# ScalarE scales the routed token rows out of place, and TensorE combines the last expert pass by selector products

## What is computed

```python
def _moe(x, router_w, wg, wu, wd):
    xf = x.reshape(b * t, d)
    logits = (xf @ router_w).astype(jnp.float32)
    top_val, top_idx = lax.top_k(logits, TOP_K)           # TOP_K = 2 of N_EXPERTS = 8
    gates = jax.nn.softmax(top_val, axis=-1)
    combine = jnp.sum(jax.nn.one_hot(top_idx, N_EXPERTS) * gates[..., None], axis=1)
    y = jnp.zeros((b * t, d), jnp.float32)
    for e in range(N_EXPERTS):
        y = y + combine[:, e:e + 1] * _swiglu(xf, wg[e], wu[e], wd[e])
    return y
...
h = h + _moe(_rmsnorm(h, norm2_g[1]), ...)
y = _rmsnorm(h, final_norm_g)
```

## Time and profile before

| what | value |
|---|---|
| median of three runs | 1635.87 us (1633.38, 1635.87, 1636.98) |
| the profiled execution, its own time | 1633.93 us |
| its span, first to last instruction | 1632.1 us |
| PE busy | 1517.0 us, 93% |
| PE weight loads | 1318.9 us, 81% |
| DVE busy | 1283.1 us, 79% |
| ACT busy | 958.9 us, 59% |
| POOL busy | 222.5 us, 14% |
| DMA | 447.74 MB, 274 GB/s over the span |
| mean granted clock of TensorE | 0.964 of full speed |

### The profile page before, as it was taken

One profiled execution on the slowest core, in us unless ns is written; L12 is line 12 of the kernel. 1 busy time (PEld: TensorE's weight loads), 2 busy tenths in 40 slices (PEclk: granted clock), 3 DMA queues, 4 the chain that ended last, 5 costly groups with the idle time before them and its releaser, 6 DMA issues.

```text
span 1632.1 us, 21551 instructions
## 1 busy us (share of the span) xinstructions
PE 1517.0 (93%) x7811; PEld 1318.9 (81%) x7811; DVE 1283.1 (79%) x1279; ACT 958.9 (59%) x903; POOL 222.5 (14%) x235
## 2 busy tenths in 40 slices
PE   4958999999996889899999999999999999999993
PEld 4857999999985887688888888888888888888882
DVE  4898765544589758788888888888888888888885
ACT  3444243333344426677777777777777777777772
POOL 4354500001135406300000000000000000000001
PEclk8979999999997988999999999999999999999997
DMA  6114699435111536999999999999999999999993
GB/s 185 34 56 152 204 325 293 147 119 174 52 33 62 168 98 202 395 396 376 372 371 366 378 366 366 373 366 373 385 349 375 375 361 366 384 364 369 385 343 114
DMA packets 243728, 447.74 MB, mean 274 GB/s; under 512 B 8869, under 2 KB 93925, under 8 KB 243679
## 3 DMA queue, kind: packets, MB, share of 16 engines
q1 hardware_dynamic: 239568, 437.35, 75.4%
q0 software_dynamic: 2880, 9.56, 1.9%
q10 hardware_dynamic: 1231, 0.19, 0.1%
HBM read 421.43 MB, written 25.65 MB: 274 GB/s over the span
## 4 chain that ended last, share of the span: by engine, by line
PE 56%; issue 4%; DVE 2%; POOL 2%; ACT 2%; DMA 1%; SPq 0%; DVEq 0%; ACTq 0%; POOLq 0%
PE ps L1479 18%; PE ps L1481 18%; PE ps L1480 18%; PE ps L1766 1%; ACT w_hi L480 1%; POOL hn L724 1%; DVE xg_lo L1408 1%; POOL xg L727 1%; PE ps L1749 1%; POOL og L760 0%; DMA xg<-hn,row_i 0%; DMA og<-obuf,out_row_i 0%; DMA raw<-in_moe_w_gate_dram 0%; DVE w_lo L485 0%; PE ps L1650 0%
## 5 line engine op out<-in xcount | busy, mean ns | idle before, releaser
L485 DVE TENSOR_TENSOR w_lo<-raw,w_hi 128x2048 fp32r<-128x2048 f32 x336 | 769.4, 2292 | 139.4 <-ACT w_hi L480 137.6
L480 ACT ACTIVATE w_hi<-raw 128x2048 fp32r<-128x2048 f32 x336 | 643.6, 1916 | 141.1 <-PE ps L1481 132.4
L1479 PE MATMUL ps<-w_hi,xg_hi 128*128 128x512 f32 x896 | 356.9, 398 | 10.1 <-DVE w_lo L485 5.4
L1480 PE MATMUL ps<-w_lo,xg_hi 128*128 128x512 f32 x896 | 355.1, 396 | 0.0
L1481 PE MATMUL ps<-w_hi,xg_lo 128*128 128x512 f32 x896 | 354.7, 396 | 0.0
L1479 PEld LDWEIGHTS ps<-w_hi,xg_hi 128*128 128x128 f32 x896 | 169.1, 189 | 53.6 <-issue 7.8
L1481 PEld LDWEIGHTS ps<-w_hi,xg_lo 128*128 128x128 f32 x896 | 169.3, 189 | 40.7
L1480 PEld LDWEIGHTS ps<-w_lo,xg_hi 128*128 128x128 f32 x896 | 169.3, 189 | 39.8
L1479 PE MATMUL ps<-x_hi,w_hi 128*128 128x336 f32 x580 | 189.0, 326 | 11.3 <-DVE x_lo L1223 5.8
L1481 PE MATMUL ps<-x_hi,w_lo 128*128 128x336 f32 x580 | 187.1, 323 | 0.0
L1480 PE MATMUL ps<-x_lo,w_hi 128*128 128x336 f32 x580 | 186.7, 322 | 0.0
(11 more groups left out here) (236 smaller groups left out, 1878.8 us busy)
## 6 DMA issues: line engine op xcount, KB each, us to landing
raw<-in_moe_w_gate_dram SPq DMA_DIRECT2D x112, 1024.0 KB, 7.2
raw<-in_moe_w_up_dram SPq DMA_DIRECT2D x112, 1024.0 KB, 7.5
raw<-in_moe_w_down_dram SPq DMA_DIRECT2D x112, 1024.0 KB, 7.1
raw<-in_w_in_dram SPq DMA_DIRECT2D x12, 1024.0 KB, 5.0
raw<-in_ffn_w_gate_dram SPq DMA_DIRECT2D x11, 1024.0 KB, 6.1
raw<-in_ffn_w_up_dram SPq DMA_DIRECT2D x11, 1024.0 KB, 6.4
raw<-in_w_out_dram SPq DMA_DIRECT2D x8, 1024.0 KB, 9.8
obuf<-ones SPq DMA_DIRECT2D x15, 512.0 KB, 7.9
```

What stands on the lines that cost most here:

```text
L480: nc.scalar.activation(hi, r, ACT.Copy).then_inc(hi_done, 1)
L485: nc.vector.tensor_tensor(lo, r, hi.bitcast(F32), ALU.subtract).then_inc(lo_done, 1)
L1479: nc.tensor.matmul(out, a_hi, b_hi, start=start, stop=False)
L1480: nc.tensor.matmul(out, a_hi, b_lo, start=False, stop=False)
```

## The change

Three things are done.

1. `hn` is no longer scaled in place by POOL. ACT writes the scaled rows to another tile (`hs`, which is `og[:, 1]`, empty until the end) by three Copy activations with the 1/rms as scale, placed between its wait for `gap_done` and the Exp. POOL's scatters read `hs` and wait for these (`hn_scaled`) and for the rows; POOL no longer waits for PE's gather.
2. The last pass's output doesn't go through `obuf`. All six gathers of line 760 are issued at `o_early`. The higher rows which are of the last pass hold nothing of use then; their gate is set to zero (`early_gate`). POOL prepares, during the passes, the position of each token's higher row in the last chunk (`last_pos`), sends it through a small DRAM row to all partitions, and compares it with the partition's number: `sel_t` is 1 where slot s of the last chunk belongs to token t. After the last pass ACT and DVE split `D_` to `o_hi` and `o_lo`, and PE multiplies them by `sel_t`: 12 products of 112 x 512 into six banks. DVE adds these, times the gate, to `yt` in six pieces.
3. DVE waits for all six gathers (`og_early` at 96) and for `sel_t` ahead of its first addition, where it waited for three; it then does the first additions (three), the two `o_lo`, three additions for the higher rows, and the six pieces.

`pick_e` moves into a free part of `h`, to make room.

```diff
@@ -123,6 +123,7 @@
 
     xg = nc.dram_tensor("xg", (CHUNKS * P, D), F32, kind="Internal").ap()
     obuf = nc.dram_tensor("obuf", ((CHUNKS + 1) * P, D), F32, kind="Internal").ap()
+    last_row = nc.dram_tensor("last_row", (T,), F32, kind="Internal").ap()
     xg_chunks = xg.rearrange("(c p) d -> c p d", p=P)
     obuf_chunks = obuf.rearrange("(c p) d -> c p d", p=P)
 
@@ -203,6 +204,7 @@
         yt = sb("yt", [TT, 3, D], F32, moe)
         hn = sb("hn", [TT, 3, D], F32, moe)
         og = sb("og", [TT, 2, 3, D], F32, moe)
+        hs = og[:, 1]
         xg_hi = sb("xg_hi", [P, KD, P], F32R, moe)
         xg_lo = sb("xg_lo", [P, KD, P], F32R, moe)
         act_s = sb("act_s", [P, 512], F32, moe)
@@ -231,6 +233,13 @@
         out_row = sb("out_row", [TT, 2, 3], F32, moe)
         out_row_i = sb("out_row_i", [TT, 2, 3], I32, moe)
         out_gate = sb("out_gate", [TT, 2, 3], F32, moe)
+        last_base = sb("last_base", [TT, 1], F32, moe)
+        last_pos = sb("last_pos", [TT, 3], F32, moe)
+        early_gate = sb("early_gate", [TT, 3], F32, moe)
+        last_bc = h[:, KD - 1, :]
+        slot_id = sb("slot_id", [P, 1], F32, moe)
+        sel_t = sb("sel_t", [P, T], F32R, moe)
+        o_hi, o_lo = (x[:].rearrange("p k s -> p (k s)") for x in (xg_hi, xg_lo))
         cnt = sb("cnt", [P, NE], F32, moe)
         extra = sb("extra", [P, NE], F32, moe)
         before_e = sb("before_e", [P, NE, NE], F32, moe)
@@ -239,7 +248,7 @@
         n_chunks = sb("n_chunks", [P, NE], F32, moe)
         key = sb("key", [P, 2, NE], F32, moe)
         pick = sb("pick", [P, 6, 2 * NE], F32, moe)
-        pick_e = sb("pick_e", [P, 6, 2 * NE], F32, moe)
+        pick_e = h[:].rearrange("p k t -> p (k t)")[:, 2 * D:2 * D + 12 * NE].rearrange("p (i e) -> p i e", i=6)
         key_sum = sb("key_sum", [P, 1], F32, moe)
         eids_f = sb("eids_f", [P, 8], F32, moe)
         table_load = sb("table_load", [1, 1], F32, moe)
@@ -249,6 +258,7 @@
         SUM_BANK, TOKEN_SUMS = ps[:, 6, 0:T], ps[0:TT, 7, 0:3]
         G_, U_, T_, X0, X1 = (ps[:, i, :] for i in (0, 1, 2, 5, 6))
         D_ = ps[:, 3:5, :]
+        LAST_BANKS = [ps[:, i, :] for i in (0, 1, 2, 5, 6, 7)]
 
 
         landed = [sem(f"landed{i}") for i in range(RAW)]
@@ -276,7 +286,7 @@
         state_stored = sem("state_stored")
         gb_landed, hn_sq = sem("gb_landed"), sem("hn_sq")
         rwg_done, logits_done, hot_done, ranks_done = sem("rwg_done"), sem("logits_done"), sem("hot_done"), sem("ranks_done")
-        gap_done, exp_done, hn_done = (sem(n) for n in ("gap_done", "exp_done", "hn_done"))
+        gap_done, exp_done, hn_done, hn_scaled = (sem(n) for n in ("gap_done", "exp_done", "hn_done", "hn_scaled"))
         sel_ready = sem("sel_ready")
         routed, extra_done = sem("routed"), sem("extra_done")
         top_done, route_step = sem("top_done"), sem("route_step")
@@ -286,9 +296,9 @@
         g_done, u_done, e_silu, e_f, t_done, ft_hi_done, ft_lo_done, d_done = (
             sem(n) for n in ("g_done", "u_done", "e_silu", "e_f", "t_done", "ft_hi_done", "ft_lo_done", "d_done"))
         o_done, o_stored, o_early = sem("o_done"), sem("o_stored"), sem("o_early")
-        o_last = [sem(f"o_last{i}") for i in (0, 1)]
-        o_last_stored, og_early = sem("o_last_stored"), sem("og_early")
-        og_late = [sem(f"og_late{t}") for t in range(3)]
+        og_early = sem("og_early")
+        last_sent, last_landed, sel_t_done = sem("last_sent"), sem("last_landed"), sem("sel_t_done")
+        o_hi_done, o_lo_done, last_done = sem("o_hi_done"), sem("o_lo_done"), sem("last_done")
         out_rows_done, y_added = sem("out_rows_done"), sem("y_added")
         fin_sq, fin_out, stored = sem("fin_sq"), sem("fin_out"), sem("stored")
         dve_step, act_step, pool_step = sem("dve_step"), sem("act_step"), sem("pool_step")
@@ -556,11 +566,6 @@
 
             sp.wait_ge(o_stored, n_pass * 16 + 16)
             sp.sem_inc(o_early, 1)
-            last_chunk = obuf_chunks[ds(n_pass, 1)].rearrange("a p d -> p (a d)")
-            for i in (0, 1):
-                sp.wait_ge(o_last[i], 1)
-                sp.dma_start(last_chunk[:, 512 * i:512 * (i + 1)], o[:, 512 * i:512 * (i + 1)]
-                             ).then_inc(o_last_stored, 16)
             n_out = 0
             for t, r, m, name, row in PIECES:
                 if name != "meta":
@@ -718,15 +723,13 @@
                 link(nc.gpsimd.tensor_tensor(out, x[:, :, 0], x[:, :, 1], ALU.add))
 
             pool.wait_ge(filled, 16 * (2 * CHUNKS + 1))
+            pool.wait_ge(hn_scaled, 3)
             pool.wait_ge(rows_done, 1)
-            pool.wait_ge(gather_done, 2)
-            for t in range(3):
-                link(nc.gpsimd.tensor_scalar(hn[:, t, :], hn[:, t, :], nt[0:TT, t, 1:2], None, ALU.mult))
             for t in range(3):
                 for k in (0, 1):
                     nc.gpsimd.indirect_dma_start(
                         out=xg, out_offset=bass.IndirectOffsetOnAxis(ap=row_i[:, t, k:k + 1], axis=0),
-                        in_=hn[:, t, :], in_offset=None).then_inc(x_sent, 16)
+                        in_=hs[:, t, :], in_offset=None).then_inc(x_sent, 16)
             pool.wait_ge(x_sent, 16 * 6)
             pool.sem_inc(x_rows, 1)
 
@@ -762,12 +765,22 @@
                     in_offset=bass.IndirectOffsetOnAxis(ap=out_row_i[:, i, t:t + 1], axis=0)).then_inc(done, 16)
 
             pool.wait_ge(out_rows_done, 1)
+            link(nc.gpsimd.tensor_scalar(last_base[:], eids_f[0:TT, 6:7], -float(P), -float(P * NE), ALU.mult, ALU.add))
+            link(nc.gpsimd.tensor_scalar(last_pos[:], out_row[:, 1, :], last_base[:, 0:1], None, ALU.add))
+            pool.dma_start(last_row.rearrange("(p t) -> p t", p=TT), last_pos[:]).then_inc(last_sent, 16)
+            link(nc.gpsimd.tensor_scalar(early_gate[:], last_pos[:], 0.0, None, ALU.is_lt))
+            link(nc.gpsimd.tensor_tensor(early_gate[:], early_gate[:], out_gate[:, 1, :], ALU.mult))
+            link(nc.gpsimd.iota(slot_id[:], pattern=[[0, 1]], base=0, channel_multiplier=1,
+                                allow_small_or_imprecise_dtypes=True))
+            pool.wait_ge(last_sent, 16)
+            pool.dma_start(last_bc, last_row.rearrange("(a t) -> a t", a=1).broadcast_to([P, T])).then_inc(last_landed, 16)
+            pool.wait_ge(last_landed, 16)
+            nc.gpsimd.tensor_scalar(sel_t[:].rearrange("s (t p) -> s t p", t=3), last_bc.rearrange("s (p t) -> s t p", t=3), slot_id[:, 0:1], None, ALU.is_equal).then_inc(sel_t_done, 1)
+
             pool.wait_ge(o_early, 1)
-            for t in range(3):
-                gather_outputs(0, t, og_early)
-            pool.wait_ge(o_last_stored, 32)
-            for t in range(3):
-                gather_outputs(1, t, og_late[t])
+            for i in (0, 1):
+                for t in range(3):
+                    gather_outputs(i, t, og_early)
 
 
         def splitter(eng, split):
@@ -935,6 +948,9 @@
             token_squares(og[:, 0], [(t, 1) for t in range(3)], lambda t, i: act.wait_ge(evac, GROUP[("htok", t, 1)] + 1), hn_sq)
 
             act.wait_ge(gap_done, 1)
+            for t in range(3):
+                act.wait_ge(hn_done, 3 + t + 1)
+                nc.scalar.activation(hs[:, t, :], hn[:, t, :], ACT.Copy, scale=nt[0:TT, t, 1:2]).then_inc(hn_scaled, 1)
             nc.scalar.activation(gt[:, :, 1], gt[:, :, 0], ACT.Exp).then_inc(exp_done, 1)
 
             def gathered_hi(p):
@@ -986,10 +1002,10 @@
                 act.nop()
             n_pass = n_over + NE
             act.wait_ge(d_done, n_pass + 1)
-            act.wait_ge(o_early, 1)
-            nc.scalar.activation(o[:, 0:512], D_[:, 0, :], ACT.Copy).then_inc(o_last[0], 1)
-            token_squares(hn, [(t, i) for t in range(3) for i in (0, 1)],
-                          lambda t, i: act.wait_ge(y_added, 2 * t + i + 4), fin_sq)
+            for i in (0, 1):
+                nc.scalar.activation(o_hi[:, 512 * i:512 * (i + 1)], D_[:, i, :], ACT.Copy).then_inc(o_hi_done, 1)
+            token_squares(hn, [(t, i) for i in (0, 1) for t in range(3)],
+                          lambda t, i: act.wait_ge(y_added, 6 + 3 * i + t + 1), fin_sq)
 
 
         @block.vector
@@ -1441,19 +1457,27 @@
                     expert_pass(i + NE)
                 dve.nop()
             n_pass = n_over + NE
-            dve.wait_ge(og_early, 48)
+            dve.wait_ge(og_early, 96)
+            dve.wait_ge(sel_t_done, 1)
             for t in range(3):
                 nc.vector.scalar_tensor_tensor(yt[:, t, :], og[:, 0, t, :], out_gate[:, 0, t:t + 1], yt[:, t, :],
                                                ALU.mult, ALU.add).then_inc(y_added, 1)
-            dve.wait_ge(d_done, n_pass + 1)
-            nc.vector.tensor_copy(o[:, 512:1024], D_[:, 1, :]).then_inc(o_last[1], 1)
-            dve.wait_ge(y_added, 3)
+            for i in (0, 1):
+                dve.wait_ge(o_hi_done, i + 1)
+                cols = slice(512 * i, 512 * (i + 1))
```

(27 more changed lines are left out.)

## The result

The changed kernel took 1622.53 us (median of four, 1621.29 to 1623.11) beside 1635.91 us for the kernel before (median of four, 1633.38 to 1636.98): ratio 0.9919, 95% interval 0.9902 to 0.9937, some 13.4 us faster. Two repeats on other occasions gave 0.9939 (0.9924 to 0.9953) and 0.9927 (0.9914 to 0.9941), that is 1625.57 and 1623.52 us; over all three comparisons the means differ by 11.3 us (15 executions at 1623.5, 24 at 1634.8, either with a standard deviation of 1.7).

A forecast was written before the change was run, and what follows sets the result against it. The prediction took TensorE, busy nearly all the time, to bound the kernel. Pass 0, ACT's copies and the end summed to -7.3 + 0 - 1.5 = -8.8 us, forecast 1626.5 us, range 1623 to 1631.5.

The forecast's parts named there:

- The pause in pass 0: Pass 0: SP's wait at `x_rows` goes, and with it PE's pause and the low clock behind it: -7.3 us.
- ACT's copies: Before pass 0: three copies, 3.4 us in all, stay hidden with 0.3 us to spare; forecast 0, bounds 0 and +1.5.
- rival (e): Scatters beside DVE's routing chain and first subtraction: POOL's issues hold DVE, pass 0 starts 12.6 us late, 1638.8 us; chance 0.05.
- the arrival T of the six gathers: At the end: all six gathers are there at 1606.4, about when PE ends; bounds 1603.2 and 1610.6.
- DVE's chain behind T: At the end: from the gathers' arrival DVE's additions, `o_lo` and six pieces take 12.8 us, ending at 1619.2.
- The end's term: After PE's last product: DVE's last addition ends at 1619.2 instead of 1620.71, -1.5 us.
- case (b): At the end: the six gathers come early, near 1603, with issues of 0.93 while DVE subtracts: 1623.7 us; chance 0.07.
- (a): At the end: the six gathers come late, behind 1607.9, losing up to 2.7 us: 1628 to 1630.5; chance 0.22.
- (c): Around pass 0: ACT is late, up to 2.4 us, or competing loads leave a short pause: 1628 to 1632; chance 0.11.

The follow-up runs named there:

- e5: The changed kernel with three further, unused copies of 112 x 1024 on ACT: 1627.55 us, ratio 0.9957.
- e6: The changed kernel, but POOL waits for the last `obuf` store, then gathers, scales and adds one group at a time to `yt` during pass 7: 1626.51 us.
- e2: The changed kernel with POOL's in-place scaling put back, so only the gathers and the end are new: 1632.16 us, ratio 0.9985.
- e1: The kernel before with only the scaling moved to ACT, the end left as it was: 1626.70 us, ratio 0.9952.
- e11: The changed kernel with three small one-column copies on POOL between its wait for `o_early` and the first gather: 1623.78 us, single execution.
- e4: The changed kernel with three further gathers ahead of the six, DVE waiting for all: 1630.73 us, single execution.

## Why the prediction held, and where it didn't

**The pause in pass 0.** Said: 7.3 us and nothing given back. Measured: 7.0 (means of two and three profiles), 7.7 in the first pair, 7.4 to 7.7 where both start at the lower clock. The cause, SP's queue behind `x_rows`, and the price of the low clock with it, were right. But my working of it had a slip that the room behind it hid: the rows were to have landed by 632.6, with the 16.4 us of before, and SP was never to stand. They take 19.4 us (616.43 to 635.86), since the last issue's data come 8.4 us behind it, beside raw loads that fill DMA (0.98 to 1.04 of its share from 624 on), where before it was 3.6 (650.79 less the 3.59 of POOL's idle time is the end of the issue), with DMA at 0.72 of its share from 644 to 648; that the loads are what delays them is the reading that fits, not tested. SP still stands, for 1.1 us here and 0.4 and 0.9 in the repeats, and tile 11 is issued at 636.60 as foreseen ("near 637"), and PE waits for none of it.

**ACT's copies.** Said: 3.4 us, 0.3 to spare. Measured: 3.23 and 0.6; e5 shows that the cover ends there. There was no pause behind a table load: Exp's load ends at 614.11 and Exp starts at 614.12, and as much holds for Silu's. The drain that the Trainium skill (ScalarE: Activation LUTs, What ACT_TABLE_LOAD costs) adds to each switch isn't seen in this kernel, at either of two.

**POOL against DVE at the scatters, rival (e).** DVE's subtraction at 618.26 takes 2.29 us beside the scatters: not held. But e6 shows that the mechanism exists, with POOL's two-input addition. The Trainium skill's exclusion (SBUF — State Buffer, SBUF: two separate sides) is thus seen in both directions here, but not for all work of POOL: an issue of POOL ends only behind DVE's subtraction, and the subtraction behind POOL's addition, while neither an issue (2.29 us beside it) nor POOL's scaling (2.62) holds the subtraction for its whole length.

**The step that failed: the arrival T of the six gathers.** It was put at 1606.4, 0.05 us behind PE's last product. It lay 2.1, 1.2 and 1.7 us ahead in three profiles of the changed kernel and 1.0 in e2. Three terms made it up. (1) The first issue starts 19.3 us ahead of PE's last product, not 18.7. The 0.6 us come with parts 2 and 3 (e2 has them, e1 doesn't): from the end of SP's last load instruction to POOL's first issue it is 2.5 us in the kernel before and e1, 2.0 in the changed kernel and e2. Why is open. (2) I took the three early issues as they stood, 2.97, 2.85 and 2.00, and added three of 2.0. But the durations belong to the phase, not to the instruction: an issue ends 0.8 to 0.9 us behind the subtraction in which it falls. 0.6 us earlier the first one starts in a pause and takes 1.04, and six end in 13.1 us instead of the 15.3 of the sum. (3) The landing behind the last issue took 4.1 to 4.9 us (5.2 in e2), not 3.4, which gave 0.7 to 1.5 back. e11 puts the phase back and gets T = +0.2 and an end of 24.1 us, the prediction's place. The rest of this part held: DVE's chain behind T is 12.5 us (12.8 said), PE's products are hidden even at half clock, the end is T + a constant (e4, e11). The rows to see the phase in were at hand in the timeline of DVE, which has the subtraction at 1587.42 beside POOL's 1587.68; I read the durations without it. The end's term was put at -1.5 us; it measured -3.3 (mean), -4.0 in the first pair.

**The range.** With T right the sum is -7.3 - 3.3 = -10.6, 1624.4 us by the mean of the four times shown, and 1622.5 lies 2 us lower. The likely rest is the wandering before the first pass (3.7 us between profiles) and of the low clock (up to 1.5): with a spread of 1.7 us for one execution, two medians of four can differ by 2 us from their long mean. My range had at its low end only case (b), with hardly any of this spread below it. Of the rivals, (a) and (c) didn't come; T went half of the way to (b) or a little more, and the end's gain with it (3.3 of the 4 us named there), but not by what (b) asked for, issues of 0.93 while DVE subtracts: the two short issues, 1.04 and 0.92, each start before a subtraction, and the four between take 2.0 to 3.0.

## What to carry to other kernels

A load queue that holds a wait in its midst stops everything behind it: look for what delays the signal, and move that work to an engine with idle time before the signal is due; the gain is the whole pause and the low clock behind it. How long POOL takes to issue an indirect transfer was set here by where the issue falls between VectorE's instructions: lay the timelines of both engines over each other before adding such durations up. A shift by 0.8 us cost up to 2.3 here. Work moved earlier is free only where its resource is idle then: the same 2.75 MB were hidden in pass 0, and cost 2.7 us in pass 7.
